# Turning k's heads on VectorE in a fused decoder layer, with attention one step later and w_o's last steps reordered

## The reference

```python
hn = rms_norm(x, norm_mix)
q, k, v = split(hn @ w_in, 3)              # w_in is 2048 x 6144
q = rms_norm(heads(q), q_gain) * 128 ** -0.5
k = rms_norm(heads(k), k_gain)             # norm over the 128 of a head
z = q @ k.T                                # strictly causal
a = exp(log_sigmoid(z) + suffix_sum_exclusive(log_sigmoid(-z)))
x = x + (a @ v) @ w_o
x = x + (silu(hf @ w_gate) * (hf @ w_up)) @ w_down        # hf = rms_norm(x, norm_ffn)
x = x + sigmoid(rms_norm(x, ple_norm) @ w_pg) * (p @ w_pp)
```

## Time and profile before

| | us |
|---|---|
| median of 3 runs | 1214.81 (1214.78 to 1214.85) |
| the profiled execution | 1214.82 |
| its span, first to last instruction | 1213.0 |
| PE busy | 1205.7 |
| DVE busy | 834.5 |
| ACT busy | 585.0 |
| GpSimd busy | 61.5 |

### The profile page before, as it was taken

The page is one execution under the profiler, slowest core; times in us unless marked ns, Lnnn a source line. Parts: engine busy times, 40 slices in busy tenths (PEclk is TensorE's granted clock), DMA queues, the critical chain, the costliest instruction groups (busy, mean ns, idle before and its releaser), DMA issues.

```text
span 1213.0 us, 15076 instructions
## 1 busy us (share of the span) xinstructions
PE 1205.7 (99%) x5446; PEld 1000.0 (82%) x5446; DVE 834.5 (69%) x1058; ACT 585.0 (48%) x727; POOL 61.5 (5%) x94
## 2 busy tenths in 40 slices
PE   9999999999999999999999999999999999999998
PEld 7888888887888888888888888888888888888886
DVE  5868678686689676676676577677666665655554
ACT  6555474655654544443443444444444444444442
POOL 0301111011000300000000000000000000002000
PEclk9999999999999999999999999999999999999999
DMA  8655565555555766766766666676565656565663
GB/s 269 209 178 175 170 187 169 183 168 172 163 169 174 222 191 179 207 194 185 205 191 181 202 193 187 189 208 191 180 204 184 205 182 208 180 204 190 209 210 102
DMA packets 119699, 229.49 MB, mean 189 GB/s; under 512 B 7218, under 2 KB 8548, under 8 KB 119652
## 3 DMA queue, kind: packets, MB, share of 16 engines
q1 hardware_dynamic: 119620, 228.90, 61.5%
q10 hardware_dynamic: 32, 0.01, 0.0%
HBM read 226.78 MB, written 2.10 MB: 189 GB/s over the span
## 4 chain that ended last, share of the span: by engine, by line
PE 67%; DVE 0%; issue 0%; DVEq 0%
PE acc L1055 67%; PE T L1088 0%; DVE stage L1019 0%; DVE x L1022 0%; DVE w_lo L696 0%; DVE side L911 0%; DVEq L1016 0%
## 5 line engine op out<-in xcount | busy, mean ns | idle before, releaser
L432 ACT ACTIVATE w_hi<-raw 128x1024 fp32r<-128x1024 f32 x425 | 448.9, 1059 | 539.1 <-PE acc L1055 528.8
L696 DVE TENSOR_TENSOR w_lo<-raw,w_hi 128x1024 fp32r<-128x1024 f32 x425 | 521.3, 1232 | 258.3 <-ACT w_hi L432 254.6
L1055 PE MATMUL acc<-w_hi,xT_hi 128*128 128x512 f32 x1204 | 471.7, 392 | 0.2
L1055 PE MATMUL acc<-w_hi,xT_lo 128*128 128x512 f32 x1204 | 468.8, 389 | 0.0
L1055 PE MATMUL acc<-w_lo,xT_hi 128*128 128x512 f32 x1204 | 468.5, 389 | 0.0
L1055 PEld LDWEIGHTS acc<-w_hi,xT_lo 128*128 128x128 f32 x1204 | 226.0, 188 | 47.5
L1055 PEld LDWEIGHTS acc<-w_hi,xT_hi 128*128 128x128 f32 x1204 | 226.0, 188 | 47.1 <-issue 1.3
L1055 PEld LDWEIGHTS acc<-w_lo,xT_hi 128*128 128x128 f32 x1204 | 226.1, 188 | 45.9
L1055 PE MATMUL acc<-w_hi,hT_hi 128*128 128x512 f32 x352 | 136.9, 389 | 0.0
L1055 PE MATMUL acc<-w_lo,hT_hi 128*128 128x512 f32 x352 | 136.9, 389 | 0.0
L1055 PE MATMUL acc<-w_hi,hT_lo 128*128 128x512 f32 x352 | 136.9, 389 | 0.0
(11 more groups left out here) (131 smaller groups left out, 582.1 us busy)
## 6 DMA issues: line engine op xcount, KB each, us to landing
raw<-in_sb_w_in SPq DMA_DIRECT2D x93, 512.0 KB, 3.7
raw<-in_ffn_w_gate SPq DMA_DIRECT2D x88, 512.0 KB, 3.7
raw<-in_ffn_w_up SPq DMA_DIRECT2D x88, 512.0 KB, 3.8
raw<-in_ffn_w_down SPq DMA_DIRECT2D x88, 512.0 KB, 4.2
raw<-in_sb_w_out SPq DMA_DIRECT2D x32, 512.0 KB, 3.8
raw<-in_ple_w_gate SPq DMA_DIRECT2D x32, 512.0 KB, 4.2
x<-in_x SPq DMA_DIRECT2D x8, 256.0 KB, 6.0
raw<-in_ple_w_proj SPq DMA_DIRECT2D x4, 512.0 KB, 6.4
```

Source lines behind the costliest of these rows:

```text
L432: act.activation(w_parts[0][:, slot(u), 0:n, :], raw[:, slot(u), 0:n, :], ACT.Copy).then_inc(hi_ready, 1)
L696: dve.tensor_tensor(w_parts[1][:, slot(u), 0:n, :], raw[:, slot(u), 0:n, :], w_parts[0][:, slot(u), 0:n, :].bitcast(F32), ALU.subtract).th ...
L1055: last = pe.matmul(acc[pair][tb][:, :], parts[a][:, c, tb * P:(tb + 1) * P], w_parts[w][:, slot(u), i, :], start=(start and i == 0 and n = ...
```

## The change

Four things change.
- k is turned by DVE, as q is: sixteen 32x256 transposes from `normed` into `k_side` (the memory of `squares` seen another way), four in each of the steps 20 to 23. PE's two rounds and all uses of `T[0]` for k go.
- ACT reads `k_side` once for `kT_hi` and once for `k0` (`k_hi`), DVE makes `kT_lo` in one operation (`k_lo`), both at step 0 of the next group. Squaring a tile now waits for `kT_ready`, since it writes the same memory.
- q's turning starts at step 14 instead of 13; `q_hi` and `q_lo` move one step too. q's norm stays at step 13 and k's at step 20.
- Attention is called with `u - 1`, so every piece of it stands one step later on all engines; the last `keep_o` falls into step 0 of w_o's second part. The last four steps of `B_HEAD` come as (tile 0, unit 6), (tile 1, unit 6), (tile 0, unit 7), (tile 1, unit 7).

```diff
-    B_HEAD = [(t, D_UNITS[u]) for t in range(2) for u in range(6)] + [(t, D_UNITS[u]) for t in range(2) for u in (6, 7)]
+    B_HEAD = [(t, D_UNITS[u]) for t in range(2) for u in range(6)] + [(t, D_UNITS[u]) for u in (6, 7) for t in range(2)]
...
-    Q_TURN, Q_UNITS, Q_HI, Q_LO = 13, 6, 20, 21
+    A_FROM, B_FROM = 1, 1
+
+    Q_NORM, Q_TURN, Q_UNITS, Q_HI, Q_LO = 13, 14, 6, 21, 22
+    K_NORM, K_TURN, K_UNITS, K_SPLIT = 20, 20, 4, 0
...
+            def k_hi(g):
+
+                act.wait_ge(k_side_ready, g + 1)
+                act.activation(kT[0][:, :, :], k_side, ACT.Copy, scale=gains[:, KG:KG + 1]).then_inc(k_hi_ready, 1)
+                act.activation(k0[:, :, :], k_side[:, :, 0:P], ACT.Copy, scale=gains[:, KG:KG + 1]).then_inc(k_hi_ready, 1)
...
                     if not first:
+                        if u == K_SPLIT:
+                            k_hi(g - 1)
                         if u == 1:
                             keep_v(g - 1, U0 - 1)
-                        attend(u, g - 1, A_EVERY)
+                        attend(u - A_FROM, g - 1, A_EVERY)
...
+            def turn_k(g, i):
+
+                if i == 0:
+                    left(dve, 1, A_P1 + g + 1)
+                    dve.wait_ge(kT_ready, g)
+                    dve.wait_ge(head_ssq_ready, 2 * g + 2)
+                for a, b in QUADRANTS[i * QN * QN // K_UNITS:(i + 1) * QN * QN // K_UNITS]:
+                    last = turn_heads(k_side, a, b)
+                if i == K_UNITS - 1:
+                    last.then_inc(k_side_ready, 1)
+
+            def k_lo(g):
+                dve.wait_ge(k_hi_ready, 2 * g + 2)
+                dve.scalar_tensor_tensor(out=kT[1][:, :, :], in0=k_side, scalar=gains[:, KG:KG + 1],
+                                         in1=kT[0][:, :, :].bitcast(F32), op0=ALU.mult,
+                                         op1=ALU.subtract).then_inc(kT_ready, 1)
...
-                    for m in range(2):
-                        if u == 2 * DU + 4 + 2 * m:
-                            left(pe, 1, A_P1 + g + 1)
-                            turn(0, normed, 2 * m, (X_ROUNDS + 1) // 2 + 2 * g + m)
```

More of the change, by code:

```diff
@@ L169, in trunk @@
             gain_rows = at_row("gain_rows", [2 * KD + 2, P])
-            squares = at("squares", [P, TB, NT])
+            squares = at_row("squares", [P, TB, NT])
+            k_side = squares[:, :, :].rearrange("p t n -> p (t n)").rearrange("p (h s) -> p h s", h=HG)
             softplus = at("softplus", [P, 3 * P])
@@ L212, in trunk @@
         qT_ready = sem("qT_ready")
+        k_side_ready = sem("k_side_ready")
+        k_hi_ready = sem("k_hi_ready")
+        kT_ready = sem("kT_ready")
         side_ready = sem("side_ready")
@@ L746, in sum_heads, with norm_heads @@
                                       ALU.mult, ALU.mult).then_inc(head_ms_ready, 1)
-            def norm_heads(n, pair, rounds, q_turned):
+            def norm_heads(n, pair, q_turned, k_turned):
                 dve.wait_ge(head_r_ready, n + 1)
-                dve.wait_ge(T_ready, X_ROUNDS + rounds)
                 dve.wait_ge(q_side_ready, q_turned)
+                dve.wait_ge(k_side_ready, k_turned)
                 for tb in range(TB):
@@ L757, in norm_heads, with turn_heads @@
                                              op0=ALU.mult, op1=ALU.mult).then_inc(acc_free[pair][tb], 1)
+            def turn_heads(to, a, b):
+                return dve.transpose(
+                    to[b * Q:(b + 1) * Q, :, :].rearrange("p h (t s) -> p t h s", t=TB)[:, :, :, a * Q:(a + 1) * Q],
+                    normed[a * Q:(a + 1) * Q, :, :].rearrange("p t (h d) -> p t h d", d=HD)[:, :, :, b * Q:(b + 1) * Q])
             def turn_q(g, i):
@@ L765, in turn_q @@
                 for a, b in QUADRANTS[i * QN * QN // Q_UNITS:(i + 1) * QN * QN // Q_UNITS]:
-                    last = dve.transpose(
-                        q_side[b * Q:(b + 1) * Q, :, :].rearrange("p h (t s) -> p t h s", t=TB)[:, :, :, a * Q:(a + 1) * Q],
-                        normed[a * Q:(a + 1) * Q, :, :].rearrange("p t (h d) -> p t h d", d=HD)[:, :, :, b * Q:(b + 1) * Q])
+                    last = turn_heads(q_side, a, b)
                 if i == Q_UNITS - 1:
                     last.then_inc(q_side_ready, 1)
[L772 to L778, removed]
+            def turn_k(g, i):
[12 more added lines that the diff above has]
+                                         op1=ALU.subtract).then_inc(kT_ready, 1)
             def keep_v(g):
@@ L857, in group @@
                     if not first:
+                        if u == K_SPLIT:
+                            k_lo(g - 1)
                         if u == 1:
                             keep_v(g - 1)
-                        attend(u, g - 1, A_EVERY)
+                        attend(u - A_FROM, g - 1, A_EVERY)
                     for part in range(2):
@@ L864, in group @@
                             sum_heads(2 * g + part)
-                        if u == end + 6 - part:
-                            norm_heads(2 * g + part, part, 2 * g, g + part)
+                        if u == (Q_NORM, K_NORM)[part]:
+                            norm_heads(2 * g + part, part, g + part, g)
                     if Q_TURN <= u < Q_TURN + Q_UNITS:
                         turn_q(g, u - Q_TURN)
+                    if K_TURN <= u < K_TURN + K_UNITS:
+                        turn_k(g, u - K_TURN)
                     if u == Q_LO:
@@ L899, in _ @@
             for u, (t, blocks) in enumerate(B_HEAD):
-                mask_scores(u, GROUPS - 1, B_EVERY)
+                mask_scores(u - B_FROM, GROUPS - 1, B_EVERY)
                 lo(B0 + u, u, len(blocks))
+                if u == K_SPLIT:
+                    k_lo(GROUPS - 1)
                 if u == 1:
                     keep_v(GROUPS - 1)
-                attend(u, GROUPS - 1, B_EVERY)
+                attend(u - B_FROM, GROUPS - 1, B_EVERY)
             def turn_side(k, i, n, pair, tiles):
@@ L940, in _ @@
                 lo(B2 + u, u, 2)
+                if u == 0:
+                    attend(BH - B_FROM, GROUPS - 1, B_EVERY)
                 tiles_of_b(u)
```

31 lines of the change are left out of this document (12 added, 19 removed).

## The result

The changed kernel takes **1232.78 us** (median of 5 runs, 1231.46 to 1234.36); the kernel before took 1214.85 beside it (1214.78 to 1214.93). The ratio is 1.0148, 95% interval [1.0138, 1.0159]: slower by 1.5%. The forecast was 1228.3. The profiled execution of after took 1233.9 us with a span of 1232.1, 1.1 above the median, and against the span of before, 1213.0, there are 19.1 us to be found.

What follows compares the result with a forecast made beforehand. PE's instruction stream was taken to bound the kernel. -3.5 + 14.6 - 1.4 + 2.2 + 1.6 = +13.5 on the span of 1213.0, plus 1.8 outside it, gave 1228.3 us (own range 1224.5 to 1231, wide range 1222 to 1234).

Steps and rivals of the forecast that it cites:

- the wait for v's tile: Before the first product of later groups and w_o, PE waits for v_lo: 3.8 + 3 x 3.6 = +14.6 us.
- The walk of VectorE: VectorE's operations at the first group's end, added from 57.79 to v_lo's end at 80.7; PE starts at about 80.85.
- Rounds, -3.5: PE loses eight rounds of four transposes of k, 0.44 us a round: -3.5 us.
- estimate of 12.5 us: Worth of the 32 transposes at the skill page's 390 ns each; the total would then be 1219.3 us.
- Weight, -1.4: PE's wait for the first head's `weight` goes, 1.34 us and 0.06 of slow restart: -1.4 us.
- w_o's order, +2.2: In w_o's first part tile 0 is done a step (2.72 us) later, less 0.55 swallowed by VectorE: +2.2 us.
- The clock, +1.6: PE's clock falls to half speed behind one of the four gaps, at 1.6 us a fall: +1.6 us.
- A: Rival: VectorE keeps up at the group boundaries and only the gains stand, 1209.9 us; chance 6%.
- C: Rival: smaller waits (4 x 3.0), w_o's order costs nothing, the clock stays up; +7.1, 1221.9 us; chance 10%.
- B: Rival: the clock falls in every gap, 4 x 1.9 instead of 1.6 us; 1234.3 us; chance 15%.

Runs made afterwards that it cites:

- e5_fill14: The changed kernel with 14 unused identity matmuls on PE ahead of the first product of groups 2 to 4 and of w_o; 1226.91 us.
- e4_order: The kernel before with only the new order of w_o's last four steps; 1216.30 us.
- e3_shift_order: The kernel before with attention one step later and the new order of w_o's last steps; 1217.75 us.
- e8_unroll: e6_early_v with PE's loop over the groups written out; 1214.04 us.
- e9_unroll_b: e8_unroll with the adding, turning and low halves of w_o's first tiles moved by a step; 1214.41 us.
- e2_vfirst: The changed kernel with v_hi ahead of k's copies on ScalarE and v_lo right behind unit 0, ahead of kT_lo, on VectorE; 1217.62 us.
- e6_early_v: As e2_vfirst, but v_hi between k's copies, kT_lo waiting for the first copy only, q turned over five steps, q_lo at step 23; 1215.47 us.
- e7_shift_old: The kernel before with attention one step later and the old order of w_o's last steps; 1218.70 us.

## Why the prediction was right, and where not

- **Direction and main term: right.** The sum's largest term was the wait for v's tile, 3.8 + 3 x 3.6 = 14.6 us; measured 3.9, 3.65, 3.65, 3.75, in all 15.0. The walk of VectorE came out piece by piece: the norm at 63.13 (forecast 62.9), the last turn's end at 76.2 (75.4 before q_lo, 76.0 with it), v_lo's end at 81.1 (80.7). PE's last product ahead of the gap started at 77.03, so PE arrived at 77.26 (77.0), and went on at 81.15 (80.85): both ends lie 0.3 late, and the gap is as forecast. The new subtraction, taken at 1.29, is 1.28; the copies, taken at 1.06 and 0.68, are 1.15 and 0.70.
- **Rounds, -3.5: right.** The starts in after and the balance, which closes to 0.3 us, both say so. The Trainium skill's page "VectorE: DVE Perf Modes" (section "The three transpose paths") has 390 ns for a 128x128 transpose of bf16 on TensorE; those here are float32. By the estimate of 12.5 us from it e5_fill14 would have come to 1217.9; it came to 1226.9.
- **Weight, -1.4: right.** The wait is in the list of e4_order, without the shift, and not in those of after and e3_shift_order, with it. It is back with 0.2 in e8_unroll and e9_unroll_b.
- **w_o's order, +2.2: too large.** Measured 1.45 (e4_order) and 1.3 (profile of after). Mechanism and place were right: DVE's turning of the tiles comes later against PE. What VectorE can swallow was undersized: I allowed 0.55 of the 2.72 us, the runs leave about 1.3. I had taken only waits; what I left out was the weight unit that the adding had stood behind and the short unit in place of one of 1.95, less a new wait for the tile's second half.
- **The clock, +1.6: the step that failed.** "I count one fall of four" was the wrong count: in the profiled execution it fell at every gap, for 17.1 us in all, and even the fastest one has by the estimate above some 7 us at half. The price of one fall was well sized (1.6; e2_vfirst and e6_early_v show 1.7 and 2.0), the count was not. The term is 5.9 us in medians and 7.4 in the profiled execution. Without it the forecast's sum is 1226.7, and e5_fill14, which has no fall, is 1226.9. That they are so close is part luck: the gaps cost 0.4 more than forecast and w_o's order 0.8 less.
- **The rivals.** A (VectorE keeps up) is out: what decides is 0.7 us at each boundary, and it was 3.75. C is out: the waits were not smaller, the order cost 1.45, and the clock fell. B (the clock falls in every gap) happened in the profiled execution, and in medians cost 5.9 for its 7.6. The median of 1232.8 lies nearer to B's 1234.3 than to the forecast's 1228.3, and above the forecast's own range, 1231; the wide range holds it only because it was drawn to reach B. Against B I had said that one event is thin. But it was the only row on the question, it said 3.1 us, and all four gaps were longer. The chance should have gone with it.

## What to carry to other kernels

Work taken off the bounding engine pays only if what it waits for next comes no later: lay out the helper's chain up to that moment in starts, and look above all at what stands in front of the one instruction that releases the bounding engine. Here reordering a few instructions without removing any moved the time by 15 us. Where a wait opens in front of TensorE, ask whether the half clock comes after it as a second cost. Here it came behind pauses of about 2 us in up to half of the runs, behind gaps of 3.7 to 3.9 us at all four in the profiled one, and behind 1.3 us not at all; each fall cost about 1.7 us. Parts of a change that look like decoration can be each other's repair: measure them alone and together.

## What the hardware showed that I had not expected

- The clock can fall behind a shorter idle time than the 3.1 us of the earlier trace rows: in e2_vfirst PE's last record ended about 298.1 and it restarted at 300.11, and from 300.78 on 3.4 us ran at half. The first line is the pause, the second what follows it (same columns as above):

```profile
298.10:300.10 2.00, 0.00 (x0) 0.00 (x0) 2.00 (x2) 1.33 (x2) 0.00 (x0) 1.00 0.53 140
300.78:304.19 3.41, 3.41 (x10) 2.63 (x9) 2.80 (x5) 1.54 (x3) 0.00 (x0) 0.50 0.92 283
```

  In half of its runs it did not fall, by their time and mean clock, and in the kernel before, with 1.3 us, it stayed at 1.00. The Trainium skill's page "TensorE: Matmul & The Clock Gate" (section "Part 1: The HAM clock gate (the "warmup" mystery)") says that idleness brings the half clock; these rows agree and add that at about 2 us it is a toss (5 of 10 runs here, 4 of 11 in e6_early_v, 1 of 5 in e7_shift_old).
- Some matmuls of no use hold the clock up (e5_fill14, 14 in a gap, 1.0), and are worth 5.9 us where the gap can't be closed.
- PE stood 1.8 to 2.0 us some fifteen matmul records behind the end of a hardware loop, with nothing that it waited for in the profile; writing the loop out removed it. Other kernels with the same loop did not have it.
- A float32 matmul of 128x128 is two records, 0.11 us from start to start (28 records for the 14 of e5_fill14). A float32 transpose of that size is one: before had 32 for k, and after has 32 records less.
